# First eight of nine chunk projections from fp32 weights and activations, low parts last, all modulation dots on VectorE

## The reference, cut to what matters

```python
mod = silu(c) @ w_ada + b_ada
sh1, sc1, g1, sh2, sc2, g2 = split(mod, 6)
h = rmsnorm(x, ln1) * (1 + sc1) + sh1
rq, rk, rv, rg, aq, ak, av = split_in(h @ w_in)
```

## Time and profile before

| | us |
|---|---|
| median of 3 runs | 1348.3 |
| lowest, highest | 1346.28, 1349.41 |
| profiled execution, time | 1346.84 |
| profiled execution, span of the trace | 1345.0 |
| TensorE busy in the span | 1252.7 (93%) |
| VectorE / ScalarE / GpSimd busy | 850.2 / 533.0 / 580.6 |
| first matmul of unit 3 (L1933) | 107.15 after the span's start |

### The profile page before, as it was taken

How to read it: one execution, slowest core, us unless ns; L and a number is a source line. 1 busy time by engine, 2 the same in 40 slices (tenths; PEclk the granted TensorE clock), 3 DMA queues, 4 the chain that set the end, 5 groups by cost and what they waited for, 6 DMA issues and landing times.

```text
span 1345.0 us, 22676 instructions
## 1 busy us (share of the span) xinstructions
PE 1252.7 (93%) x8609; PEld 1193.2 (89%) x8609; DVE 850.2 (63%) x1495; ACT 533.0 (40%) x1074; POOL 580.6 (43%) x352
## 2 busy tenths in 40 slices
PE   5479999999999999779999999999999999999995
PEld 2468898988988899779999999999999999998995
DVE  6976648558376735997666666666666368772305
ACT  5563434344345432444333333333333322334422
POOL 4852113032142342345535435354352587765770
PEclk9799999999999999899999999999999999999998
DMA  9412222223033423202232222322221898685971
GB/s 368 163 35 82 88 73 78 70 86 111 27 116 110 133 68 114 98 32 97 99 126 100 98 97 99 123 102 101 96 99 76 305 356 318 224 315 193 339 257 45
DMA packets 74394, 185.56 MB, mean 138 GB/s; under 512 B 7425, under 2 KB 39745, under 8 KB 74049
## 3 DMA queue, kind: packets, MB, share of 16 engines
q1 hardware_dynamic: 72640, 183.63, 38.0%
q10 hardware_dynamic: 1664, 0.72, 0.2%
HBM read 150.14 MB, written 34.19 MB: 137 GB/s over the span
## 4 chain that ended last, share of the span: by engine, by line
PE 69%; DVE 12%; POOL 5%; issue 5%; DMA 5%; ACT 3%; SPq 0%; DVEq 0%; ACTq 0%; PEldq 0%; POOLq 0%
PE bank L2198 32%; PE bank L1933 13%; PE bank L2238 10%; PE bank L2174 5%; DMA w_raw<-in_w_units 3%; POOL w_more L1346 2%; PE bank L2045 2%; POOL w_extra L1346 1%; DVE ada_out L1383 1%; DVE std L1570 1%; PE bank L2015 1%; PE bank L2030 1%; POOL w_hl L1307 1%; DMA xm<-in_x_t 1%; PE bank L2079 1%
## 5 line engine op out<-in xcount | busy, mean ns | idle before, releaser
L1933 PE MATMUL bank<-act_hl,w_hl 128*128 128x362 f32 (+1 forms) x1368 | 256.6, 336 | 0.1
L1933 PEld LDWEIGHTS bank<-act_hl,w_hl 128*128 128x128 f32 x1368 | 223.3, 188 | 9.3 <-issue 7.1
L1204 POOL TENSOR_TENSOR w_hl<-w_raw,w_hl 128x1024 fp32r<-128x1024 f32 x24 | 57.2, 2387 | 259.9 <-ACT w_hl L721 259.9
L2238 PE MATMUL bank<-u_hl,w_more 128*128 128x362 f32 (+1 forms) x672 | 116.6, 332 | 2.7 <-POOL w_more L1346 2.3
L2198 PE MATMUL bank<-x_blocks_a,w_hl 128*128 128x272 f32 x864 | 113.7, 290 | 4.8 <-issue 4.8
L2238 PEld LDWEIGHTS bank<-u_hl,w_more 128*128 128x128 f32 x672 | 113.5, 191 | 3.8 <-POOL w_more L1346 3.2
L2198 PEld LDWEIGHTS bank<-x_blocks_a,w_hl 128*128 128x128 f32 x864 | 111.4, 190 | 5.3 <-issue 5.0
L2198 PE MATMUL bank<-x_blocks_b,w_hl 128*128 128x272 f32 x864 | 112.7, 288 | 2.0 <-ACT x_blocks_b L1014 1.7
L2198 PE MATMUL bank<-x_blocks_a,w_ext 128*128 128x272 f32 x840 | 110.5, 290 | 2.8 <-POOL w_ext L1307 1.8
L2198 PEld LDWEIGHTS bank<-x_blocks_b,w_hl 128*128 128x128 f32 x864 | 109.8, 188 | 2.9 <-DVE up_b L1680 1.3
L2198 PEld LDWEIGHTS bank<-x_blocks_a,w_ext 128*128 128x128 f32 x840 | 107.9, 190 | 3.4 <-POOL w_ext L1307 2.4
(11 more groups left out here) (241 smaller groups left out, 2371.1 us busy)
## 6 DMA issues: line engine op xcount, KB each, us to landing
w_raw<-in_w_units SPq DMA_DIRECT2D x142, 512.0 KB, 4.3
ada_w<-in_w_ada_t SPq DMA_DIRECT2D x36, 512.0 KB, 3.9
u_hl<-u_dram SPq DMA_DIRECT2D x44, 362.0 KB, 5.5
u_dram<-acc SPq DMA_DIRECT2D x22, 544.0 KB, 2.7
u_dram<-up_b SPq DMA_DIRECT2D x22, 544.0 KB, 2.7
ada_d<-in_w_ada_t SPq DMA_DIRECT2D x16, 512.0 KB, 5.2
u_hl<-u_dram SPq DMA_DIRECT2D x22, 364.0 KB, 8.3
xm<-in_x_t SPq DMA_DIRECT2D x2, 1448.0 KB, 13.6
```

Of the source, the lines that this page charges most:

```text
L1204: pool.tensor_tensor(w_hl[:, slot, 1], w_raw[:, slot], w_hl[:, slot, 0].bitcast(F32), ALU.subtract).then_inc(wl_ready, 1)
L1933: ins = pe.matmul(bank[c][:, 0:m], w_hl[:, slot, w, k, :], act_hl[:, x, k, a:a + m], start=(pas == 0 and i == 0), stop=(pas == 2 and i == ...
L2238: ins = pe.matmul(bank[o][:, 0:m], w_down(q)[:, w, o, :], u_hl[:, q % U_RING, x, 0:m], start=(f == pas == 0), stop=(f == FT - 1 and pas == 2))
```

## The change

- The first three weight units are loaded as they are into `w_first` (in the place of `w_hl`), and not split. TensorE multiplies them in fp32 with `xm` itself, one fp32 matmul for three fp32r ones (`first_product`).
- VectorE scales all three chunks of x in place (`scale_x`), and ScalarE adds the shift, once as the high part into `act_hl`, once in place (`shift_x`). The order of the items is `X_ORDER`: k-tiles 0 to 2 chunk by chunk, then k by k.
- GpSimd does nothing in this part. The low parts of h are made by VectorE in eight instructions of 1088 columns (`x_lo`) when everything is scaled; unit 3 waits for them.
- All 16 modulation tiles are dots of VectorE, in 11 places. The four small tables come right behind the third chunk of x in the queue of SP, the identity has a semaphore of its own, and the three weight units follow modulation tile 7.
- TensorE takes the last k-tile only when all its chunks are ready. The ninth product is eight fp32 matmuls, with all nine transposes of the values behind it.

The diff, cut to its core:

```diff
+ADA_LOADS = tuple(range(11))
+ADA_PLACE = {m: m % 11 for m in range(16)}
+X_ORDER = ([(0, 0), (1, 0), (0, 1), (1, 1), (2, 0), (2, 1), (0, 2), (1, 2), (2, 2)]
+           + [(k, c) for k in range(3, KT) for c in range(3)])
...
+        first_units_phase = ExitStack()
+        w_first = sb("w_first", [P, 3, 2, KT, P], at=first_units_phase)
+        first_units_phase.close()
...
             def load_first_ada(m):
-                if 12 <= m < 14:
-                    sp.dma_start(ada_pool_place[m - 12], w_ada[m]).then_inc(ada_pool_loaded[m - 12], 16)
-                    return
-                nth = ADA_DVE.index(m)
-                if nth >= 7:
-                    sp.wait_ge(ada_used, 2 * (nth - 7) + 2)
-                sp.dma_start(ada_place[nth % 7], w_ada[m]).then_inc(ada_loaded[nth % 7], 16)
+                place = ADA_PLACE[m]
+                if m > 10:
+                    sp.wait_ge(ada_used, 2 * (place + 1))
+                sp.dma_start(ada_place[place], w_ada[m]).then_inc(ada_loaded[place], 16)
...
+            def load_first_unit(n):
+
+                slot = SLOTS[n]
+                sp.dma_start(w_first[:, slot, 0], w_units[n].rearrange("p (k m) -> p k m", k=KT)).then_inc(
+                    first_loaded[n], 16)
+                sp.sem_inc(w_loaded[slot], 16)
...
-            load_first_ada(12)
             load_first_ada(4)
             load_first_ada(5)
             load_x(2)
-            load_unit(0, [0])
+            for dst, src in ((b_ada_sb, b_ada), (gains_sb, gains), (conv_wb_sb, conv_wb), (conv_st_sb, conv_st)):
+                sp.dma_start(dst[:], src).then_inc(const_loaded, 16)
+            sp.dma_start(ident[:], ident_in).then_inc(ident_loaded, 16)
             load_first_ada(6)
-            load_unit(1, [1])
-            load_unit(2, [2])
-            for dst, src in ((b_ada_sb, b_ada), (gains_sb, gains), (ident, ident_in), (conv_wb_sb, conv_wb),
-                             (conv_st_sb, conv_st)):
-                sp.dma_start(dst[:], src).then_inc(const_loaded, 16)
-            for m in (7, 8, 13, 9, 10, 11, 14, 15):
+            load_first_ada(7)
+            for n in range(3):
+                load_first_unit(n)
+            for m in range(8, 16):
...
+            def shift_x(k, c):
+
+                act.wait_ge(x_scaled, X_ORDER.index((k, c)) + 1)
+                for in_place in (False, True):
                     for o, tok, m, part in pieces(c):
-                        slot = H_RING[item % 5][:, o:o + m]
-                        src = xm[:, k, tok:tok + m] if c == 0 else slot
-                        ins = act.activation(slot if ring else act_hl[:, 0, k, tok:tok + m], src, ACT.Identity,
-                                             bias=mod[:, 2 * k + 1, part:part + 1],
-                                             scale=1.0 if c else scale_n[:, 0, k, part:part + 1])
+                        x = xm[:, k, tok:tok + m]
+                        ins = act.activation(x if in_place else act_hl[:, 0, k, tok:tok + m], x, ACT.Identity,
+                                             bias=mod[:, 2 * k + 1, part:part + 1])
                 ins.then_inc(hi_ready, 1)
...
-            def split_hf(item, c, k, ring=None):
-
-                a, n = CHUNKS[c]
-                pool.wait_ge(hi_ready, item + 1)
-                h = hf[:, item % 3] if ring is None else ring[item % 5]
-                pool.tensor_tensor(act_hl[:, 1, k, a:a + n], h[:, 0:n],
-                                   act_hl[:, 0, k, a:a + n].bitcast(F32), ALU.subtract).then_inc(lo_ready, 1)
...
-            def multiply_ada(m, s):
-
-                if s == 0 and m > 12:
-                    pool.wait_ge(ada_summed, 2 * (m - 12) - 1)
-                pool.wait_ge(ada_pool_loaded[m - 12], 16)
-                dst = ada_pool_place[m - 12] if s else acc[:, 0:D]
-                pool.tensor_tensor(dst, ada_pool_place[m - 12], silu_c[:, s], ALU.mult).then_inc(ada_product, 1)
-
-            pool.wait_ge(silu_c_ready, 1)
-            for s in range(2):
-                multiply_ada(12, s)
-
-            pool.wait_ge(x_inv_ready, 1)
-            for k in range(KT):
-                x = xm[:, k, 0:CHUNKS[0][1]]
-                pool.tensor_tensor(x, x, std[:, 0], ALU.mult).then_inc(x_normed, 1)
-            for n in range(3):
-                split_weights(n, [n])
-            for k in range(KT):
-                for c in range(3):
-                    split_hf(3 * k + c, c, k, H_RING)
-                if k in (1, 3):
-                    multiply_ada(13, k // 2)
+            pool.sem_inc(wl_ready, 3)
...
+                if k == 0:
+                    dve.wait_ge(const_loaded, 16 * 4)
+                then_wait(add_ada_bias(m, 2, m + 2, m % 12))
                 dve.tensor_scalar(scale_n[:, 0, k, :], mod[:, 2 * k, :], 1.0, gains_sb[:, 0, k:k + 1],
                                   ALU.add, ALU.mult).then_inc(vec_ready, 1)
                 dve.wait_ge(vec_ready, k + 1)
 
-
-            dve.wait_ge(silu_c_ready, 1)
-            for m in range(7):
-                first_ada_dots(m)
-                if m in (3, 5):
-                    invert(m // 2 - 1, m // 2 - 1)
-                if m == 3:
-                    dve.sem_inc(x_inv_ready, 1)
-            invert(2, 2)
-            dve.wait_ge(const_loaded, 16 * 5)
-
-            dve.wait_ge(sq_used, 3 * KT)
-            for k in range(KT):
-                first_vectors(k)
-                for c in (1, 2):
-                    item = 3 * k + c
-                    if item >= 5:
-                        dve.wait_ge(lo_ready, item - 4)
+            def scale_x(*parts):
+
+                for k, c in parts:
                     for o, tok, m, part in pieces(c):
-                        ins = dve.scalar_tensor_tensor(H_RING[item % 5][:, o:o + m], xm[:, k, tok:tok + m],
-                                                       scale_n[:, 0, k, part:part + 1], std[:, c, o:o + m],
+                        x = xm[:, k, tok:tok + m]
+                        ins = dve.scalar_tensor_tensor(x, x, scale_n[:, 0, k, part:part + 1], std[:, c, o:o + m],
                                                        ALU.mult, ALU.mult)
                     ins.then_inc(x_scaled, 1)
-                    for tile in ADA_DOTS_IN.get(k, ())[c - 1:c]:
-                        first_ada_dots(tile)
-
-            dve.sem_inc(ada_used, 4)
-            dve.wait_ge(x_scaled, 2 * KT)
-            dve.wait_ge(x_normed, KT)
+
+            def x_lo(k):
+
+                dve.tensor_tensor(act_hl[:, 1, k, :], xm[:, k, :], act_hl[:, 0, k, :].bitcast(F32),
+                                  ALU.subtract).then_inc(lo_ready, 1)
+
+            dve.wait_ge(silu_c_ready, 1)
+            for m in range(4):
+                first_ada_dots(m)
+            invert(0, 0)
+            first_vectors(0)
+            scale_x((0, 0))
+            first_vectors(1)
+            scale_x((1, 0))
+            first_ada_dots(4)
+            first_ada_dots(5)
+            invert(1, 1)
+            scale_x((0, 1), (1, 1))
+            first_vectors(2)
+            scale_x((2, 0), (2, 1))
+            invert(2, 2)
+            scale_x((0, 2), (1, 2), (2, 2))
+            for k in range(3, KT):
+                first_ada_dots(2 * k)
+                first_ada_dots(2 * k + 1)
+                first_vectors(k)
+                scale_x(*[(k, c) for c in range(3)])
+
+            dve.wait_ge(x_scaled, 3 * KT)
             dve.sem_inc(norm_applied, 3)
...
+            dve.wait_ge(hi_ready, 3 * (KT - 1))
+            for k in range(KT - 1):
+                x_lo(k)
+            dve.wait_ge(hi_ready, 3 * KT)
+            x_lo(KT - 1)
...
+            def first_product(u, c, k, at):
+
+                a, m = CHUNKS[c]
+                ins = pe.matmul(at[:, 0:m], w_first[:, SLOTS[u], 0, k, :], xm[:, k, a:a + m], start=(k == 0),
+                                stop=(k == KT - 1))
+                if k == KT - 1:
+                    ins.then_inc(gemm_ready, 1)
+
+            for u in range(3):
+                pe.wait_ge(first_loaded[u], 16)
             pe.wait_ge(std_ready, 3)
-            for k in range(KT):
-                jobs = [(u, c) for c in range(3) for u in range(3) if (u, c) != (2, 2)]
-                for u, c in sorted(jobs) if k == KT - 1 else jobs:
-                    a, m = CHUNKS[c]
-                    pe.wait_ge(lo_ready, 3 * k + c + 1)
-                    for pas, (w, x) in enumerate(((0, 0), (0, 1), (1, 0))):
-                        ins = pe.matmul(bank[3 * u + c][:, 0:m], w_hl[:, SLOTS[u], w, k, :], act_hl[:, x, k, a:a + m],
-                                        start=(k == pas == 0), stop=(k == KT - 1 and pas == 2))
-                    if k == KT - 1:
-                        ins.then_inc(gemm_ready, 1)
+            for i, (k, c) in enumerate(X_ORDER[:3 * (KT - 1)]):
+                pe.wait_ge(hi_ready, i + 1)
+                for u in range(3 if c < 2 else 2):
+                    first_product(u, c, k, bank[3 * u + c])
```

(10 more changed lines are left out.)

74 lines of the change are left out of this document (18 added, 56 removed).

## The result

The changed kernel takes 1338.5 us (median of four runs, 1336.6 to 1338.9) beside 1347.5 of the kernel before (median of four, 1346.3 to 1349.4). The ratio is 0.993 with a 95% interval of 0.9916 to 0.9943, so it is faster by 0.6 to 0.8%. The forecast was 1339.8 with a range of 1335.5 to 1344.0: right in direction, and 1.3 us too high. Of these, some 0.8 us lie in what it started from, a median of 1348.3 from three runs, which is 1347.5 with a fourth. The profiled execution took 1338.92 us with a span of 1337.1, against 1345.0 before.

A forecast was written before the change was run, and what follows sets the result against it. VectorE's dots and scalings, slowed beside GpSimd, were taken to bound the entry. Unit 3 moving from 107.15 to 96.3 gains 10.9 us, less 2.4 for the clock is 8.5: profiled 1338.3, median 1339.8, range 1335.5 to 1344.

The forecast's parts named there:

- What bounds the kernel: Entry up to unit 3: VectorE's dots and scalings are the chain, TensorE waits; an earlier unit 3 counts one for one.
- Tables: VectorE's first vectors wait for four small tables, there at 25.8 us; bounds 23.4 (no wait) and 31.7.
- VectorE's k-tile: k = 3 to 7: two tiles, vectors and three chunks take 7.44 us each, so VectorE's scaling ends at 79.7.
- fp32 product: TensorE's fp32 product of 362 columns costs 0.61 us, 4.9 for a k-tile of eight, hidden behind VectorE's 7.44.
- the bound of 1.3: Upper bound in us on one fp32 product on TensorE, from the first two sums, read as the lower clock level.
- rival 3: TensorE becomes the bound; slower from 0.945 us a product, 1368 us at the lower clock throughout; chance 0.03.
- Tail without the clock: From VectorE's end at 79.7 through shift, last products, ScalarE's step, ninth product and transposes: unit 3 at 96.3, 10.9 us gained.
- now 7.5: Tail's ninth product and nine transposes up to unit 3: 7.5 us, against 6.7 before.
- Clock: After 5 us idle, TensorE's last k-tile begins at 1.2 GHz; loss of 2.4 us, between 0 and 3.0.
- As before: Everything after unit 3's start takes the same time as in the earlier kernel; no loss there.
- over 2 us in hand: Margin of VectorE's low parts (done at 90) before the transposes' copies (wanted at 93.9), even if GpSimd's split slows two.

The follow-up runs named there:

- e3: Changed kernel with the four small tables loaded ahead of the third chunk of x; 1334.9 us, unit 3 starts at 94.36.
- e8: Changed kernel with every product of k-tiles 3 to 6 followed by one of the same size with zero weights; 1344.5 us, unit 3 at 103.51.
- e5: Changed kernel with the ninth product waiting only for its own bank's eviction, not for seven; 1330.2 us, unit 3 at 94.57.
- f1: Changed kernel with tables first, ninth product behind its own bank's eviction, last k-tile chunk by chunk, ScalarE evicting in that order; 1331.6 us.
- e1: Changed kernel with 16 extra 128x1024 multiplications on GpSimd from about 21 us, results unused; 1360.6 us, unit 3 at 123.97.
- e2: Changed kernel with the eight low parts of h made by GpSimd beside the dots, not by VectorE at the end; 1352.8 us.

## Why the prediction was right, point by point

- **What bounds the kernel** was right: the chain up to the last k-tile is VectorE's, and the entry moved.
- **Tables.** Forecast 25.8, measured 26.38. e3 shows that the wait is on the path in full.
- **VectorE's k-tile.** Forecast 7.44, measured 7.29; end 79.7 against 79.2. Every dot took 1.22 or 1.23 without GpSimd beside it, so the duration taken from the earlier trace rows held.
- **fp32 product.** Forecast 0.61, measured 14.87 for 24 without a gap, 0.62. It is hidden, since TensorE waits for VectorE before each k-tile from 3 on, and e8 shows what it costs when it is not. The price that the Trainium skill in Perfetto Trace Analysis (Engine Utilization) would give, 0.30 by estimate, is refuted by this row of weights that do real work. One reading of the forecast does not hold: it took the 2.77 us of the first two sums for the lower level of the clock, but the granted clock of that stretch (12.5 to 15.0) is 1.00. Why they were slow stays open; the bound of 1.3 and the time of rival 3 rest on half the clock, which the k-tiles of 6.84 us do show.
- **Tail without the clock.** Last shift 81.5 (forecast 82.1). ScalarE's step ahead of the ninth product 1.03 (1.7, as part of the evictions ran beside the products). The transposes 3.2 (2.7: from the second on they go in pairs every 0.71, not every 0.65 for each of the two banks, and the last of them starts 0.43 before unit 3, not 0.1). The two misses nearly cancel, which is luck. (The forecast's "now 7.5" is 7.6 by its own terms, 4.9 and 2.7.)
- **Clock.** The mechanism was right: idle for 4.46 us, then a clock of 0.67. The size was not: 1.7 us (6.84 less 5.15) against 2.4. The granted clock was still 1.00 during the idle time (77.1 to 81.5) and at the lower level for 3.4 us behind it, where the forecast had read some 6 us out of the earlier trace rows. This term (with the products, 6.84 instead of 7.3), ScalarE's step and the earlier shift, less the longer transposes, make the entry 97.65 instead of 98.7. Whether it falls in this k-tile at all differs between executions: in e5 it fell one k-tile earlier.
- **After unit 3.** "As before" is true of the head units (341.7 us from first to last start in both) and not shown for the rest. From unit 3's start to the end of the span it took 1237.85 before and 1239.45 after, but over all fourteen kernels, whose stages there are the same, this ranges from 1233.8 to 1239.5, whatever the entry is. The 1.6 us lie within that. So that the median came within 1.3 us of the forecast is closer than the argument could promise; the entry, 97.65 against 98.7, is the better test of it. It is also why e5 stands at 1330.2 with an entry 3.6 us behind f1's. Where these 6 us come from was not tried.
- **The reason for the gain** was right, its size wrong, though no term of the sum used it. I read the earlier trace rows as "1.86 instead of 1.23, a factor of 1.5", and expected too little of e1 and e2, by 10 and 6 us from the upper ends. The true price is a wait for the rest of one GpSimd instruction, per VectorE instruction, and the row at 40.08 of the kernel before (2.27 us for two elements) had it. In the forecast the factor was the cover of "over 2 us in hand" for the low parts: in the changed kernel the split starts at 89.11, when VectorE's low parts end at 89.09, and so the question did not come up. In f1 it did, and cost VectorE 2.16 us where I would have said 1.3; some 1.3 of them reached the entry, as the transposes waited 1.61 us instead of 0.28.
